# The output projection of a hybrid decoder trunk: seven block products in place of eight, accumulated in PSUM

## The chip, the cores and the metric

The kernel runs on one core of a Trainium2 chip. The metric is the device time of one execution in microseconds (us); lower is better. TensorE (PE), VectorE (DVE), ScalarE (ACT), GpSimd (POOL) and SyncE (SP, which here only issues transfers) work in order, each on its own queue, and wait for each other by semaphores.

## What is computed

Two layers (DEPTH = 2) over 1024 tokens of width 1024, all in float32. The part that matters, cut from the reference:

```python
for l in range(DEPTH):
    ...
    merged = jax.nn.sigmoid(gate_a) * y_a + jax.nn.sigmoid(gate_b) * y_b
    x = x + g1 * (merged @ w_out[l])
    h = rms_norm(x, norm2_g[l]) * (1.0 + sc2) + sh2
    x = x + g2 * ((jax.nn.silu(h @ w_gate[l]) * (h @ w_up[l])) @ w_down[l])
return rms_norm(x, final_g)
```

`merged @ w_out` is a 1024 x 1024 by 1024 x 1024 product. `c_act @ w_ada[l]` (the adaLN modulation) is computed for the next layer while the present one runs.

## The kernel before

Activations are held transposed: 128 channels on the partitions, tokens along the row, as 8 tiles of 128 x 1024 (KT = 8, HALF = 512 tokens). A float32 product is made of three passes of rounded operands: each operand is split into a high part (ScalarE's copy to a rounded type) and a low part (the remainder, by a subtraction on GpSimd for weights and mostly on VectorE for activations), and `products` (L707 to 712) issues high x high, high x low and low x high into one PSUM bank of 128 x 512.

**Merge.** For each of 8 channel tiles the two branch outputs come from 48 matmuls into four PSUM banks. VectorE multiplies them by the gates, which SP loads per tile (L1040), and adds them to `m_sum`; ScalarE makes `mg_hi` of it, VectorE `mg_lo`.

**Output projection** (units U_OUT to U_OUT+7). A unit is one tile of 128 output channels: SP loads its weights (L704), ScalarE splits off the high part (L685), GpSimd the low part (L693), one unit ahead. TensorE runs 8 inner tiles x 2 halves of the tokens x 3 passes = 48 matmuls a unit, 384 in all, two units alternating between PSUM banks 0 and 1, and 2 and 3. After each unit VectorE adds the bank pair, times g1, to `x_sb` (L2926). In layer 0 it then makes two or three of the 16 row reductions for the next layer's modulation (L2453), whose rows SP loads by ROWS_BEHIND. ScalarE squares the updated x (L1924), GpSimd sums the squares (L1183). The last two units run half by half: first both first halves, then both second halves, so that the norm of the first half (`mean_squares` L1394 on TensorE, the root on ScalarE, the reciprocal on VectorE, `norm_scale` L1403 on TensorE) is made under the second halves.

**Entry of the FFN.** The first gate and up products (`first_up`) take h of the first half as VectorE makes it, channel tile by channel tile (`hidden_scaled` L2570, `hidden_lo` L2581); the mean squares of the second half stand between them.

**Down projection.** Near the end of a layer the product with w_down already runs as seven products over 11 pairs of blocks, 77 steps of 12 matmuls each. Weights and hidden blocks, with their sums made earlier, are loaded step by step (SP, L1099 and L1112), split through a ring of three slots (`d_hi_lo`; copies L1912 on ScalarE, low halves on GpSimd L666 and VectorE L2441) and accumulated into 8 PSUM banks; `down_evictions` (from L3090) spreads the accumulations into x behind VectorE's low halves by a list of step numbers.

All orders are written out by hand, engine by engine; a counter a semaphore says how many instructions of a kind are done.

## Time and profile before

| what | value |
|---|---|
| median of 3 runs | 2896.54 us (2896.39 to 2897.36) |
| profiled execution | 2895.48 us |
| its span | 2893.6 us |
| granted TensorE clock, mean | 0.995 |
| busy: PE, DVE, ACT, POOL | 2829.5, 2103.5, 1223.9, 1253.3 us |

The profiled execution is one run beside the three; its span runs from the first to the last instruction, and its time has another 1.9 us around it. Busy times are sums over an engine's instructions: matmuls are pipelined, so the 0.39 us of a matmul's row is not the distance to the next. In the rows below "L709" is line 709 of the kernel, `out<-in` are the program's buffer names, "[1.57 <-PE ps L712]" is the idle time ahead of an instruction and what ended it, and PEclk is the granted TensorE clock as a share of 2.4 GHz.

### The profile page before, as it was taken

To read this page: it belongs to the slowest core of one execution; us is meant where nothing else is said; L and a number is where in the kernel's file an instruction comes from. 1 tells how busy PE (TensorE), PEld (TensorE's weight loads), DVE (VectorE), ACT (ScalarE), POOL (GpSimd) and SP (SyncE) were. 2 spreads that over 40 slices of the span, in tenths; PEclk is the share of its full clock that TensorE was granted. 3 is DMA by queue.
4 is the path that set the end of the run, shared out by engine and by line. 5 is a ranking of instruction groups with operands and counts; after the bars stand their busy time and mean duration, and the time that the engine had idled before them with its cause. 6 is when DMAs were issued, how large, how long until landed. Compare 5 with 4: busy or idle time off the path is not lost.

```text
span 2893.6 us, 38026 instructions
## 1 busy us (share of the span) xinstructions
PE 2829.5 (98%) x13924; PEld 2386.9 (82%) x13924; DVE 2103.5 (73%) x2575; ACT 1223.9 (42%) x1965; POOL 1253.3 (43%) x834
## 2 busy tenths in 40 slices
PE   6999999999999999999999999999999899999998
PEld 6888889988877888888878888898888788888887
DVE  7998688865687777757668896788533878776665
ACT  3433377762242333344542335778313333233443
POOL 0354322242535555554625452223223555555454
PEclk9999999999999999999999999999999999999999
DMA  7565400224615544466635652011351345544665
GB/s 293 166 195 177 152 16 13 51 50 155 223 51 192 169 170 164 153 199 217 198 131 160 186 177 74 17 23 41 106 175 44 122 158 174 180 163 155 196 196 167
DMA packets 332745, 408.59 MB, mean 141 GB/s; under 512 B 52369, under 2 KB 242961, under 8 KB 328338
## 3 DMA queue, kind: packets, MB, share of 16 engines
q1 hardware_dynamic: 290128, 298.41, 34.0%
q10 hardware_dynamic: 42434, 107.77, 10.0%
q8 instruction: 111, 1.82, 0.3%
q14 instruction: 72, 0.59, 0.1%
HBM read 299.33 MB, written 104.40 MB: 140 GB/s over the span
## 4 chain that ended last, share of the span: by engine, by line
PE 86%; DVE 6%; ACT 3%; DMA 2%; POOL 1%; issue 1%; SPq 0%; ACTq 0%; DVEq 0%; POOLq 0%
PE ps L709 15%; PE ps L711 15%; PE ps L712 15%; PE ps L1775 9%; PE ps L1777 9%; PE ps L1776 9%; PE ps L1635 4%; PE ps L1616 2%; PE ps L1656 2%; PE ps L1655 2%; PE ps L1621 2%; PE ps L1620 2%; DMA raw<-in_w_b_out 1%; DVE h_lo L2581 1%; DMA ada_rows<-in_w_ada 1%
## 5 line engine op out<-in xcount | busy, mean ns | idle before, releaser
L655 POOL TENSOR_TENSOR wlo<-blocks,whi 128x512 fp32r<-128x512 f32 x288 | 430.3, 1501 | 378.0 <-ACT whi L649 375.2
L693 POOL TENSOR_TENSOR wlo<-raw,whi 128x1024 fp32r<-128x1024 f32 (+4 forms) x156 | 236.4, 1532 | 706.3 <-ACT whi L685 706.2
L649 ACT ACTIVATE whi<-blocks 128x512 fp32r<-128x512 f32 x288 | 180.4, 627 | 316.9 <-PE ps L1777 254.1
L2441 DVE TENSOR_TENSOR d_hi_lo<-blocks,d_hi_lo 128x512 fp32r<-128x512 f32 x154 | 204.3, 1330 | 140.7 <-ACT d_hi_lo L1912 140.4
L666 POOL TENSOR_TENSOR d_hi_lo<-w_pair,d_hi_lo 128x512 fp32r<-128x512 f32 x148 | 203.4, 1377 | 199.4 <-ACT d_hi_lo L1912 199.4
L709 PE MATMUL ps<-h_hi,whi 128*128 128x512 f32 x832 | 281.6, 401 | 7.0 <-DVE h_lo L2581 5.5
L711 PE MATMUL ps<-h_lo,whi 128*128 128x512 f32 x832 | 274.5, 393 | 0.0
L712 PE MATMUL ps<-h_hi,wlo 128*128 128x512 f32 x832 | 273.4, 391 | 0.0
L685 ACT ACTIVATE whi<-raw 128x1024 fp32r<-128x1024 f32 (+4 forms) x162 | 106.9, 699 | 353.0 <-PE ps L712 292.3
L1775 PE MATMUL ps<-h_hi,whi 128*128 128x512 f32 x640 | 249.5, 390 | 5.3 <-issue 3.2
L1777 PE MATMUL ps<-h_hi,wlo 128*128 128x512 f32 x640 | 249.1, 389 | 0.0
L1776 PE MATMUL ps<-h_lo,whi 128*128 128x512 f32 x640 | 249.0, 389 | 0.0
L709 PE MATMUL ps<-d_hi_lo 128*128 128x512 f32 x616 | 240.4, 390 | 2.6 <-DVE d_hi_lo L2441 2.4
L711 PE MATMUL ps<-d_hi_lo 128*128 128x512 f32 x616 | 239.7, 389 | 0.0
L712 PE MATMUL ps<-d_hi_lo 128*128 128x512 f32 x616 | 239.7, 389 | 0.0
L1775 PE MATMUL ps<-e_hi,whi 128*128 128x512 f32 x480 | 187.7, 391 | 6.4 <-POOL wlo L655 6.4
L2441 DVE TENSOR_TENSOR pt_lo<-ps,pt_hi 128x512 fp32r<-128x512 f32 x256 | 164.6, 685 | 39.8 <-ACT pt_hi L1912 39.2
L709 PEld LDWEIGHTS ps<-h_hi,whi 128*128 128x128 f32 x832 | 154.2, 190 | 41.0 <-DVE h_lo L2581 9.8
L1777 PE MATMUL ps<-e_hi,wlo 128*128 128x512 f32 x480 | 187.2, 390 | 0.0
L1776 PE MATMUL ps<-e_lo,whi 128*128 128x512 f32 x480 | 187.2, 390 | 0.0
L712 PEld LDWEIGHTS ps<-h_hi,wlo 128*128 128x128 f32 x832 | 157.3, 189 | 34.0
L711 PEld LDWEIGHTS ps<-h_lo,whi 128*128 128x128 f32 x832 | 157.7, 190 | 33.2
(338 smaller groups left out, 6888.4 us busy)
## 6 DMA issues: line engine op xcount, KB each, us to landing
blocks<-hidden_scratch SPq DMA_DIRECT2D x154, 256.0 KB, 3.7
ada_raw<-in_w_ada SPq DMA_DIRECT2D x64, 512.0 KB, 4.2
raw<-in_w_in SPq DMA_DIRECT2D x92, 256.0 KB, 4.6
w_pair<-in_w_down SPq DMA_DIRECT2D x22, 1024.0 KB, 6.2
sums_scratch<-w_pair ACTq DMA_DIRECT2D x22, 1024.0 KB, 3.9
w_pair<-sums_scratch SPq DMA_DIRECT2D x88, 256.0 KB, 3.3
blocks<-in_w_gate SPq DMA_DIRECT2D x84, 256.0 KB, 3.2
blocks<-in_w_up SPq DMA_DIRECT2D x84, 256.0 KB, 3.0
```

The costliest lines, as they stand in the source:

```text
L649: act.activation(block_view(whi, s), blocks[:, r, :], ACT.Copy).then_inc(block_hi.sem, 1)
L655: pool.tensor_tensor(block_view(wlo, s), blocks[:, r, :], block_view(whi, s).bitcast(F32), ALU.subtract)\
L666: eng.tensor_tensor(d_tile(n, 0, 1), w_pair[:, n % 4, :], d_tile(n, 0, 0).bitcast(F32), ALU.subtract)\
L693: last = pool.tensor_tensor(dst(wlo[:, s, :]), src(raw[:, s, :]), dst(whi[:, s, :].bitcast(F32)), ALU.subtract)
L709: pe.matmul(o, w_h, x_h, start=first, stop=False, skip_group_check=added)
L711: pe.matmul(o, w_h, x_l, start=False, stop=False, skip_group_check=added)
L712: return [pe.matmul(o, w_l, x_h, start=False, stop=last, skip_group_check=added) for o, (x_h, _) in zip(outs, xs)]
L1635: last = pe.transpose(ps[:, 4 + t, k * P:(k + 1) * P], probs[:, T % 2, kt * P:(kt + 1) * P], ident[:, 0:P])
L1775: pe.matmul(bank, w_h, x_h, start=opens and j == 0, stop=False, skip_group_check=added)
L1776: pe.matmul(bank, w_h, x_l, start=False, stop=False, skip_group_check=added)
L1777: end = pe.matmul(bank, w_l, x_h, start=False, stop=(j == 3), skip_group_check=added)
L2441: return dve.tensor_tensor(out, value, hi.bitcast(F32), ALU.subtract)
```

## The change

The product merged @ w_out is cut into blocks of 128 inner rows by 512: pairs of inner tiles (OPAIRS = 4) give a11, a21, a12, a22 for the weights and b11, b12, b21, b22 for the merged activations. Seven products of sums of blocks (P1 to P7, in the order of OUT) replace the eight of blocks. Each product has a step per pair, n = 0 to 27, of 4 output tiles x 3 passes = 12 matmuls. Products accumulate into bank sets 0 to 3 or 4 to 7 (OUT_BANK), some into what the product before left there (those not in OUT_OPENS), and VectorE adds a bank to x between them (`out_eviction`).

- SP loads the four weight pairs during the merge; GpSimd makes the 16 weight sums there; VectorE makes the sums of the activations per merge tile. The plain blocks a11 are loaded behind the merge's last gates, a12 and a22 later.
- Steps 0 to 3 use the old weight slots; from step 4 on weights and activations pass through rings of three (`ow_ring`, `oh_ring`): ScalarE's copies of step n wait for TensorE's step n-3, GpSimd makes the low half of the weights, VectorE that of the activations.
- Squares of x and their sums, the mean squares and the norm's scale move to other places between the steps, and the first FFN products interleave the two units evenly.
- The next layer's 16 modulation reductions of layer 0 move to the down projection, behind every third step; SP loads their rows there.

The diff, cut to its core:

```diff
+    OPAIRS = KT // 2
+    OSTEPS = 7 * OPAIRS
+    OUT = ("P1", "P5", "P6", "P3", "P7", "P2", "P4")
+    OUT_HIDDEN = {"P5": 0, "P6": 1, "P3": 2, "P7": 3, "P2": 4, "P4": 5}
+    OUT_BANK = {"P1": 0, "P6": 0, "P7": 0, "P4": 0, "P5": 4, "P3": 4, "P2": 4}
+    OUT_OPENS = ("P1", "P5", "P2")
+    ADA_STEPS = 12
...
+        def out_weight(n):
+
+            p, j = divmod(n, OPAIRS)
+            name = OUT[p]
+            if name in ("P1", "P2"):
+                return raw[:, j // 2, (j % 2) * HALF:(j % 2 + 1) * HALF]
+            if name == "P4":
+                return out_a22[j // 2][:, j % 2, :]
+            return out_pair[j][:, {"P6": 0, "P7": 1, "P3": 2, "P5": 3}[name], :]
...
+                for j in range(OPAIRS):
+                    if j % 2 == 0:
+                        sp.wait_ge(w_lo_done.sem, w_lo_done.at(l, U_MERGE + KT - 1 + j // 2))
+                        apart(sp)
+                    load_out_block(j, 0, 0, raw_part(j))
...
+                def weight_sums(j):
+
+                    a11, a21, a12, a22 = (out_pair[j][:, n, :] for n in range(4))
+                    pool.wait_ge(wo_loaded.sem, wo_loaded.at(l, 16 * OPAIRS))
+                    pool.tensor_tensor(a22, a21, a22, ALU.add).then_inc(wo_sum.sem, 1)
+                    pool.tensor_tensor(a21, a11, a21, ALU.subtract).then_inc(wo_sum.sem, 1)
+                    pool.wait_ge(wo_sum.sem, wo_sum.at(l, 4 * j + 1))
+                    pool.tensor_tensor(a11, a22, a11, ALU.subtract).then_inc(wo_sum.sem, 1)
+                    pool.wait_ge(wo_sum.sem, wo_sum.at(l, 4 * j + 3))
+                    pool.tensor_tensor(a12, a12, a11, ALU.subtract).then_inc(wo_sum.sem, 1)
...
                 for n in range(1, KT):
                     split_lo(pool, l, U_MERGE + n)
-                split_lo(pool, l, U_OUT)
-                split_lo(pool, l, U_OUT + 1)
-                for n in range(KT - 2):
-                    split_lo(pool, l, U_OUT + n + 2)
-                    if n:
-                        for t in range(2):
-                            add_squares(l, 1, t, n)
-                add_squares(l, 1, 0, KT - 2)
-                add_squares(l, 1, 0, KT - 1)
-                split_lo(pool, l, U_FFN)
-                add_squares(l, 1, 1, KT - 2)
-                add_squares(l, 1, 1, KT - 1)
+                    if n >= 4:
+                        weight_sums(n - 4)
+                for n in range(OSTEPS):
+                    pool.wait_ge(wo_hi.sem, wo_hi.at(l, wo_hi_number(n, 0)))
+                    pool.tensor_tensor(ow_tile(n, 1), out_weight(n), ow_tile(n, 0).bitcast(F32), ALU.subtract)\
+                        .then_inc(wo_lo_w.sem, 1)
+                    if 21 <= n < 25:
+                        add_squares(l, 1, 0, n - 20)
+                    if n == 25:
+                        split_lo(pool, l, U_FFN)
+                split_lo(pool, l, U_FFN + 1)
+                for k in range(1, KT):
+                    add_squares(l, 1, 1, k)
...
+                def out_step(n):
+
+                    p, j = divmod(n, OPAIRS)
+                    if j == 0:
+                        if p < 2:
+                            wait(pe, mg_free, l, KT - 1 + p)
+                        else:
+                            pe.wait_ge(wo_ev.sem, wo_ev.at(l, 4 * (p - 1)))
+                    pe.wait_ge(wo_lo_w.sem, wo_lo_w.at(l, n + 1))
+                    if n < OPAIRS:
+                        pe.wait_ge(mg_ready.sem, mg_ready.at(l, n + 1))
+                    else:
+                        pe.wait_ge(wo_lo_h.sem, wo_lo_h.at(l, n - OPAIRS + 1))
+                    for m in range(4):
+                        end = out_product(n, m)
+                        if m == 3:
+                            end.then_inc(wo_used.sem, 1)
+                        elif n in (6 * OPAIRS - 1, 7 * OPAIRS - 1):
+                            end.then_inc(wo_end.sem, 1)
+                        if n == 6 * OPAIRS and m == 1:
+                            pe.wait_ge(wo_ev.sem, wo_ev.at(l, 20 + 3))
+                            mean_squares(l, 2)
+
+                for n in range(OSTEPS):
+                    out_step(n)
+                    if n == 6 * OPAIRS:
+                        norm_scale(l, 2)
...
+                def wo_hi_part(n):
+
+                    p, j = divmod(n, OPAIRS)
+                    if n < OPAIRS:
+                        act.wait_ge(wo_loaded.sem, wo_loaded.at(l, 2 * 16 * OPAIRS))
+                        wait(act, unit_used, l, U_MERGE + KT - 1 + n // 2)
+                    elif n < OPAIRS + 3:
+                        wait(act, unit_used, l, U_MERGE + KT)
+                    else:
+                        act.wait_ge(wo_used.sem, wo_used.at(l, n - 2))
...
+                    copy(ow_tile(n, 0), out_weight(n)).then_inc(wo_hi.sem, 1)
+                    if n >= OPAIRS:
+                        copy(oh_tile(n, 0), out_hidden(n)).then_inc(wo_hi.sem, 1)
+
+                def out_square(t, k):
+
+                    act.wait_ge(wo_ev.sem, wo_ev.at(l, (12, 20)[t] + k + 1))
+                    square(l, 1, t, k)
...
+                for n in range(2, 27):
+                    wo_hi_part(n)
+                    if 19 <= n < 23:
+                        out_square(0, n - 19)
+                    if n in (23, 24):
+                        for k in range(2):
+                            out_square(0, 2 * (n - 21) + k)
+                    if n == 25:
+                        split_hi(act, l, U_FFN)
                 norm_std(l, 2)
...
+                OUT_EVICTIONS = {8: ((0, 0), (0, 1)), 9: ((0, 2), (0, 3)), 11: ((1, 0),), 12: ((1, 1),), 13: ((1, 2), (1, 3)),
+                                 14: ((2, 0),), 15: ((2, 1),), 16: ((2, 2),), 17: ((2, 3),),
+                                 18: ((3, 0),), 19: ((3, 1),), 20: ((3, 2),), 21: ((3, 3),),
+                                 22: ((4, 0), (4, 1)), 23: ((4, 2), (4, 3))}
...
+                for n in range(OPAIRS, OSTEPS - 2):
+                    out_hidden_low(n)
+                    if n in (8, 11):
+                        wait(dve, x_back[n // 11], l, 16)
+                    for p, m in OUT_EVICTIONS.get(n, ()):
+                        out_eviction(p, m)
+                    if n == 24:
+                        squares_added(0, 5)
+                squares_added(0, 6)
+                squares_added(0, 7)
+                for m in range(4):
+                    out_eviction(5, m, True)
+                out_hidden_low(OSTEPS - 2)
                 norm_inverse(l, 2)
...
+                    if l + 1 < DEPTH and n >= ADA_STEPS and n % 3 == 0 and n < ADA_STEPS + 6 * KT:
+                        at = (n - ADA_STEPS) // 3
+                        if at == 0:
+                            wait(dve, c_loaded, l, 32)
+                        ada_product(l, 4 * KT + at, at // KT, next_raw, next_c)
```

The orders on VectorE and ScalarE change in places that the diff shows only as conditions. **VectorE from the first ring steps on (layer 0)**; `oh_ring<-mg_raw` is a low half, `x_sb<-ps` an accumulation of a finished bank. Before:

```order
L2926 SCALAR_TENSOR_TENSOR x_sb<-ps,mod,x_sb 128x1024 [waits x_back_first,unit_used]
L2453 ISA next_raw,mod<-next_raw,next_c 128x1024 [waits c_loaded,ada0_loaded]
L2453 ISA mod 128x1
L2453 ISA next_raw,mod<-next_raw,next_c 128x1024 [waits ada1_loaded]
L2453 ISA mod 128x1
```

Now:

```order
L2564 TENSOR_TENSOR oh_ring<-mg_raw,oh_ring 128x512 [waits wo_hi_then_block_hi_then_d_hi] x5
L3075 SCALAR_TENSOR_TENSOR x_sb<-ps,mod,x_sb 128x512 [waits wo_used_then_plain_done_then_d_used,x_back_first]
L3075 SCALAR_TENSOR_TENSOR x_sb<-ps,mod,x_sb 128x512 [waits wo_used_then_plain_done_then_d_used]
L2564 TENSOR_TENSOR oh_ring<-mg_raw,oh_ring 128x512 [waits wo_hi_then_block_hi_then_d_hi]
L3075 SCALAR_TENSOR_TENSOR x_sb<-ps,mod,x_sb 128x512 [waits wo_used_then_plain_done_then_d_used] x2
L2564 TENSOR_TENSOR oh_ring<-mg_raw,oh_ring 128x512 [waits wo_hi_then_block_hi_then_d_hi] x2
```

The first group of five low halves is for steps 4 to 8; P1's four accumulations stand two behind the low half of step 8 and two behind that of step 9.

**VectorE around the start of P4 (steps 24 to 27)**; `sq_sum` is a sum of squares. Before, at the end of the projection:

```order
L2467 TENSOR_TENSOR mod<-mod,cols 128x8 [waits ada_used] x2
L2938 SCALAR_TENSOR_TENSOR a_57<-mod,cols 128x8 [waits mod_ready]
L2967 SCALAR_TENSOR_TENSOR x_sb<-ps,mod,x_sb 128x512 [waits out_half] x2
L2558 RECIPROCAL rstd<-std 128x4 [waits std_ready]
L2967 SCALAR_TENSOR_TENSOR x_sb<-ps,mod,x_sb 128x512 [waits unit_used]
```

Now:

```order
L2564 TENSOR_TENSOR oh_ring<-mg_raw,oh_ring 128x512 [waits wo_hi_then_block_hi_then_d_hi]
L3101 TENSOR_TENSOR sq_sum<-sq_sum,sq_ring 128x512 [waits sq0_added,sq0_ready]
L2564 TENSOR_TENSOR oh_ring<-mg_raw,oh_ring 128x512 [waits wo_hi_then_block_hi_then_d_hi]
L3101 TENSOR_TENSOR sq_sum<-sq_sum,sq_ring 128x512 [waits sq0_added,sq0_ready] x2
L3075 SCALAR_TENSOR_TENSOR x_sb<-ps,mod,x_sb 128x512 [waits wo_ev_then_w_pair_sum_then_d_ev,wo_end] x3
L3075 SCALAR_TENSOR_TENSOR x_sb<-ps,mod,x_sb 128x512 [waits wo_ev_then_w_pair_sum_then_d_ev,wo_used_then_plain_done_then_d_used]
L2564 TENSOR_TENSOR oh_ring<-mg_raw,oh_ring 128x512 [waits wo_hi_then_block_hi_then_d_hi]
L2681 RECIPROCAL rstd<-std 128x4 [waits std_ready]
L2564 TENSOR_TENSOR oh_ring<-mg_raw,oh_ring 128x512 [waits wo_hi_then_block_hi_then_d_hi]
```

The low halves here are of steps 24, 25, 26 and 27; VectorE took over three of the sums of squares, and P2's four accumulations stand behind them and behind the low half of step 25.

**ScalarE over steps 23 to 27**; `ow_ring` and `oh_ring` are the two copies of a step, `sq_ring` a square. Before, for the last units:

```order
L685 ACTIVATE whi<-raw 128x1024 [waits unit_used,raw1_loaded]
L1924 ACTIVATE sq_ring<-x_sb 128x512 [waits sq0_added,wo_ev]
L1924 ACTIVATE sq_ring<-x_sb 128x512 [waits sq1_added]
L1924 ACTIVATE sq_ring<-x_sb 128x512 [waits sq0_added,wo_ev] x2
L1946 ACT_TABLE_LOAD
```

Now:

```order
L2006 ACTIVATE ow_ring<-raw 128x512 [waits wo_loaded,wo_used_then_plain_done_then_d_used]
L2006 ACTIVATE oh_ring<-mg_raw 128x512
L2018 ACTIVATE sq_ring<-x_sb 128x512 [waits sq0_added,wo_ev_then_w_pair_sum_then_d_ev] x2
L2006 ACTIVATE ow_ring<-out_a_low 128x512 [waits wo_used_then_plain_done_then_d_used]
L2006 ACTIVATE oh_ring<-mg_raw 128x512
L2018 ACTIVATE sq_ring<-x_sb 128x512 [waits sq0_added,wo_ev_then_w_pair_sum_then_d_ev] x2
L2006 ACTIVATE ow_ring<-out_a_low 128x512 [waits wo_used_then_plain_done_then_d_used]
L2006 ACTIVATE oh_ring<-mg_raw 128x512
L734 ACTIVATE whi<-raw 128x1024 [waits wo_used_then_plain_done_then_d_used,raw0_loaded]
```

Two squares now stand between the copies of step 23 and those of 24, and two more ahead of those of 25. A square waits until the square two earlier, which used its ring slot, is in the sum.

## Rows read from the trace of the kernel before

**Rows 1.** The page's chain that ended last, by engine.

```profile
PE 86%; DVE 6%; ACT 3%; DMA 2%; POOL 1%; issue 1%; SPq 0%; ACTq 0%; DVEq 0%; POOLq 0%
```

**Rows 2.** Windows by stage: merge, out, FFN entry, down, layer 1's out.

```profile
core 0: us, PE busy (x) PEld busy (x) DVE busy (x) ACT busy (x) POOL busy (x), PEclk, DMA share, GB/s
638.00:725.00 87.00, 86.93 (x384) 71.67 (x383) 45.92 (x33) 19.02 (x18) 20.12 (x9) 1.00 0.47 154
725.00:814.00 89.00, 89.00 (x402) 73.94 (x401) 56.52 (x56) 22.13 (x30) 51.27 (x21) 1.00 0.62 199
814.00:885.00 71.00, 64.19 (x277) 50.57 (x276) 61.40 (x74) 31.30 (x52) 31.05 (x21) 0.98 0.25 84
1250.00:1440.00 190.00, 189.43 (x837) 156.57 (x836) 124.43 (x110) 89.70 (x156) 106.02 (x77) 1.00 0.70 217
2139.00:2228.00 89.00, 89.00 (x402) 73.95 (x401) 21.27 (x21) 22.13 (x30) 35.95 (x21) 1.00 0.31 101
```

**Rows 3.** Timeline of PE, layer 0's out stage: start, us, what.

```profile
724.92 0.62 PE L709 MATMUL ps<-mg_hi,whi 128*128 128x512 f32 x2
...
804.48 0.95 PE L1394 MATMUL ps<-columns,sq_sum 128*128 128x1 f32 x8
805.29 0.49 PE L709 MATMUL ps<-mg_hi,whi 128*128 128x512 f32 x1
...
813.85 0.39 PE L709 MATMUL ps<-h_hi,whi 128*128 128x512 f32 x1
```

**Rows 4.** Timeline of all engines, one step of the down projection.

```profile
1338.67 0.39 PE L709 MATMUL ps<-d_hi_lo 128*128 128x512 f32 x1
...
1338.93 0.63 ACT L1912 ACTIVATE d_hi_lo<-w_pair 128x512 fp32r<-128x512 f32 x1 [1.57 <-PE ps L712]
...
1339.64 1.29 POOL L666 TENSOR_TENSOR d_hi_lo<-w_pair,d_hi_lo 128x512 fp32r<-128x512 f32 x1 [1.43 <-ACT d_hi_lo L1912]
...
1340.12 1.36 DVE L2441 TENSOR_TENSOR d_hi_lo<-blocks,d_hi_lo 128x512 fp32r<-128x512 f32 x1 [1.36 <-ACT d_hi_lo L1912]
...
1341.59 0.75 DVE L3085 SCALAR_TENSOR_TENSOR x_sb<-ps,mod,x_sb 128x512 f32<-128x512 f32 x1
```

**Rows 5.** SP's timeline, then DMA GB/s over 705 to 726 us.

```profile
716.79 0.81 SPq L1040 DMA_DIRECT2D gl<-gate_scratch  x2
...
GB/s 0 0 0 133 148 382 273 390 460 314 312 344 207 32 0 0 0 0 0 0 0 0 0 0 156 335 304 312 406 395 259 260 258 349 311 363 358 296 327 247
```

**Rows 6.** Timeline of POOL: one sum of squares, alone.

```profile
799.99 1.29 POOL L1183 TENSOR_TENSOR sq_sum<-sq_sum,sq_ring 128x512 f32<-128x512 f32 x1 [1.43 <-ACT sq_ring L1924]
```

**Rows 7.** Weight splits on POOL, reductions on DVE; their group over 725:814.

```profile
726.26 2.40 POOL L693 TENSOR_TENSOR wlo<-raw,whi 128x1024 fp32r<-128x1024 f32 x1 [8.48 <-ACT whi L685]
...
737.20 3.50 POOL L693 TENSOR_TENSOR wlo<-raw,whi 128x1024 fp32r<-128x1024 f32 x1 [8.54 <-ACT whi L685]
...
738.36 3.42 DVE L2453 CUSTOM_DVE_ANT_0 next_raw<-next_raw,next_c 128x1024 f32<-128x1024 f32 x1
...
L2453 DVE CUSTOM_DVE_ANT_0 next_raw<-next_raw,next_c 128x1024 f32<-128x1024 f32 x16 | 33.5, 2123 | 2.7 <-DMA next_raw<-in_w_ada 2.7
```

**Rows 8.** PE behind its longest waits in the FFN entries, and windows there.

```profile
872.61 0.76 PE L1775 MATMUL ps<-e_hi,whi 128*128 128x512 f32 x1 [3.18 <-POOL wlo L655]
...
2286.59 0.47 PE L1775 MATMUL ps<-e_hi,whi 128*128 128x512 f32 x1 [3.20 <-POOL wlo L655]
...
873.00:875.00 2.00, 2.00 (x6) 1.52 (x6) 2.00 (x2) 0.00 (x0) 2.00 (x2) 0.50 0.90 356
2287.00:2290.00 3.00, 3.00 (x15) 2.47 (x14) 3.00 (x3) 0.00 (x0) 3.00 (x3) 1.00 0.87 304
```

**Rows 9.** FFN entry: mean squares on PE, first second-half h on DVE.

```profile
819.20 0.95 PE L1394 MATMUL ps<-columns,sq_sum 128*128 128x1 f32 x8
...
824.63 1.41 DVE L2570 SCALAR_TENSOR_TENSOR t_late<-x_sb,a,ps 128x512 f32<-128x512 f32 x2 [1.37 <-PE ps L1403]
```

**Rows 10.** Timeline of DVE near step 29 of the down projection.

```profile
1328.41 2.44 DVE L3085 SCALAR_TENSOR_TENSOR x_sb<-u_part,mod,x_sb 128x512 f32<-128x512 f32 x2
```

More of the change, by code:

```diff
@@ L440, in trunk @@
         h_ready = count("h_ready", 4 * KT)
-        out_half = count("out_half", 2)
+        wo_end = count("wo_end", 6)
         pcol_ready = count("pcol_ready", 1)
@@ new lines, in _ @@
+                for j in range(OPAIRS):
+                    if j % 2 == 0:
+                        sp.wait_ge(w_lo_done.sem, w_lo_done.at(l, U_MERGE + KT - 1 + j // 2))
+                        apart(sp)
+                    load_out_block(j, 0, 0, raw_part(j))
+                sp.wait_ge(wo_loaded.sem, wo_loaded.at(l, 2 * 16 * OPAIRS))
+                wait(sp, unit_used, l, U_MERGE + KT)
+                apart(sp)
+                for j in range(OPAIRS):
+                    sp.wait_ge(wo_lo_w.sem, wo_lo_w.at(l, j + 1))
+                    apart(sp)
+                    load_out_block(j, 0, 1, raw_part(j))
@@ new lines, in _ @@
+                sp.wait_ge(mg_comb.sem, mg_comb.at(l, 4 * OPAIRS))
+                apart(sp)
+                for j in range(OPAIRS):
+                    load_out_block(j, 1, 1, out_a22[j // 2][:, j % 2, :])
+                for n in range(2):
+                    sp.wait_ge(wo_lo_w.sem, wo_lo_w.at(l, 5 * OPAIRS + 2 * n + 2))
+                    apart(sp)
+                    up_unit(n)
+                sp.wait_ge(wo_lo_w.sem, wo_lo_w.at(l, 3 * OPAIRS + 4))
+                apart(sp)
+                for name in PLAIN_BLOCKS:
+                    load_block(name, 1)
@@ L1727, in _ @@
                     end[1].then_inc(unit_used.sem, 1)
-                for n in range(KT - 2):
-                    unit_ready(pe, l, U_OUT + n)
-                    wait(pe, wo_ev, l, n - 1)
-                    for k in range(KT):
-                        if n == 0:
-                            wait(pe, mg_ready, l, KT if k == KT - 1 else KT - 1)
-                        end = tile_products(pe, n % 2, 2 * (n % 2), mg_hi, mg_lo, [(k, k)],
-                                            first=(k == 0), last=(k == KT - 1))
-                    end[1].then_inc(unit_used.sem, 1)
@@ L2243, in _ @@
+                table(ACT.Sqrt)
+                for n in range(2):
+                    wo_hi_part(n)
+                wait(act, unit_used, l, U_MERGE + KT)
                 wait(act, x_spilled, l, 16)
[L2244 removed]
+                for part, tiles in enumerate((slice(0, 4), slice(4, KT))):
                     act.dma_start(x_sb[:, tiles, :], xs_dram[:, tiles, :]).then_inc(x_back[part].sem, 16)
[L2246 to L2254 removed]
@@ L3187, in _ @@
                     down_evictions(n)
+                    if l + 1 < DEPTH and n >= ADA_STEPS and n % 3 == 0 and n < ADA_STEPS + 6 * KT:
[3 more added lines that the diff above has]
+                        ada_product(l, 4 * KT + at, at // KT, next_raw, next_c)
+                    if l + 1 < DEPTH and n == 60:
+                        for m in range(2):
+                            modulation(l, 4 + m, m, cols[:, l + 1, m * KT:(m + 1) * KT])
+                        wait(dve, mod_ready, l, 6)
+                        apart(dve)
+                        dve.scalar_tensor_tensor(a1[:, :], mod[:, 1, :], 1.0, cols[:, l + 1, ROW_N1:ROW_N1 + KT],
+                                                 ALU.add, ALU.mult).then_inc(a1_ready.sem, 1)
                     if l + 1 < DEPTH and n in (40, 42):
```

308 lines of the change are left out of this document (168 added, 140 removed).

## The prediction

> **What bounds the kernel now.** I read the page's chain first [rows 1]: TensorE holds 86% of the chain that ended last. Then the windows by stage [rows 2]: in the output projection (725 to 814 in layer 0, 2139 to 2228 in layer 1) TensorE is busy in 89.00 of 89 us, both times with 402 instructions. The matmul timeline [rows 3] prices it: the first product of the stage starts at 724.92, the first of the next stage at 813.85, 88.93 later. A matmul starts every 0.2267 us (the merge runs its 384 in 87 us, [rows 2]); the 0.39 of a row is latency, not pace. 384 of them are 87.05, the two insertions for the norm 0.81 each (804.48 to 805.29, and one like it): 88.67 of the 88.93. The stage has no wait to remove. Only fewer matmuls shorten it, and any new wait of TensorE lengthens it one for one.
>
> Two more views matter. The down projection already runs seven block products through a ring of three, and shows the rhythm of a step [rows 4]. The entry of the FFN (814 to 885) is the one stage where TensorE idles (64.19 busy of 71, [rows 2]).
>
> **The change, part by part (per layer).**
> *Matmuls.* 28 steps of 12 are 336 for 384: 48 x 0.2267 = **-10.88**.
>
> *Rhythm of a step.* With S the start of a step (1338.67), ScalarE's two copies for the step two later start at S+0.26, GpSimd's low half ends at S+2.26, VectorE's low half, held back until GpSimd is through, at S+2.81, and an accumulation into x behind it takes 0.75 [rows 4], or 0.67 apart in a row (two like it in 1.41, [rows 9]). A step lasts 2.72, so low halves come 2.6 before they are needed. Inside a product nothing is lost; that cover is 2.6 and no more.
>
> *Sums of weight blocks.* 16 x 1.29 (a 128x512 subtraction, [rows 4]) = 21 on GpSimd, which is busy 20 of 87 us in the merge [rows 2]: cost 0. Without that cover the merge's weight splits would be late. VectorE's combinations, three of 1.36 at most in a tile of 10.9 us, fit beside its 46 busy of 87.
>
> *Start.* The four A11 blocks stand on SP's queue behind the last gates. Those issue from 716.79 for 0.81 [rows 5]; 1 MB of gates and 1 MB of blocks at some 320 GB/s (the middle of that answer's bandwidth row) end near 724.4. ScalarE (0.63) and GpSimd (1.29) follow, so step 0 starts near 726.5: **+1.5** (0 to 2.5). Before, the first weights had landed long since.
>
> *Banks.* Steps 8, 12, 16 and 20 may start only when four accumulations of an earlier product are done, and VectorE's queue has the last of them behind the low half of a *later* step (9, 13, 17, 21). The low half of step 9 ends at S(7)+2.81; two accumulations behind it end at S(7)+4.07, where step 8 was due at S(7)+2.72: 1.40 lost with the hand-over of 0.05. Step 12 loses the same; steps 16 and 20, with one accumulation behind, 0.74 each: **+4.3** (2.8 to 5).
>
> *Start of P4 (step 24), the largest term.* After half of step 24 TensorE waits for the third accumulation of P2 and the whole sum of squares, then writes the mean squares. Squares and sums are now threaded between steps on three queues. Count from S(19)=0; steps 20 to 24 are due at 3.46, 6.18, 8.90, 11.62, 14.34. GpSimd adds square 1 behind low half 21, to 4.10 (1.29 alone, [rows 6]); only then may ScalarE (0.63 for 128x512, [rows 4]) overwrite the ring slot, so copies 22 start at 4.69, not 3.72. The next rounds: add 2 ends 8.53, low half 23 9.82, add 3 11.66, square 5 12.34, low half 24 14.24 (VectorE's 14.79, so step 24 starts 0.5 late), add 4 16.08, VectorE's add 5 16.85, square 7 17.5. Copies 25 stand behind square 7: 17.45 to 18.62, VectorE's low half 20.00. Behind *that* on VectorE stand adds 6 and 7 and the four accumulations of P2. TensorE reaches the wait at 16.21. If VectorE's work comes in a row, the third accumulation ends at 23.2, a wait of 7.0. But GpSimd asks at 19.65 for the split of the next weights, and two such instructions take turns: GpSimd's split from 737.20 took 3.50 instead of 2.40, and VectorE's reduction issued at 738.36 took 3.42, ending 1.08 after GpSimd did [rows 7]. So split to 22.40, add 6 to 22.95, low half 26 to 24.24, add 7 to 24.80, third accumulation 26.8: a wait of 10.6. I take turns, as those rows do: **+11.1** with the 0.5 (7.5 to 12.5).
>
> *Clock.* After a wait of 3.18 us in layer 0 the granted clock was 0.50 (1.2 GHz) from 873 to 875: six matmuls at half pace, 6 x 0.2 = 1.2 us lost; after 3.20 in layer 1 it stayed 1.00 (2.4 GHz) [rows 8]. The new wait is longer than either: **+1.2** (0 to 1.7).
> The Trainium skill (TensorE: Matmul & The Clock Gate, "What's actually happening") says that an idle array falls to 1.2 GHz and rises again only after it has been kept busy, which speaks against any change that trades matmuls for one long wait. By it both layers pay, as in my sum; by the layer 1 row alone the forecast would be 2.4 less.
>
> *Entry of the FFN.* Before, most squares of the second half of the sequence were added while the last tiles ran; mean squares started 5.35 after the stage (819.20) and the first second-half h at 10.78 (824.63) [rows 9]. Now all seven adds follow the last weight split on GpSimd, in turns with VectorE's low halves of h. The same count from S(25), with the stage's end at 8.16, ends these adds at 8.8, 10.8, 12.1, 14.0, 15.9, 17.7 and 19.6; mean squares wait until 11.4 after the stage, then 0.81, root and reciprocal 0.4, the matmuls queued ahead 1.36, scale 0.8, first h at 14.9. From there VectorE sets the pace as before: **+4.1** (2 to 6).
>
> *Once, in layer 0.* The 16 reductions for the next layer (33.5 of VectorE, [rows 7]) leave a stage where they were free for the down projection, where VectorE has 124 busy of 190 [rows 2]. On a plain step one costs nothing (low half 0.3 late, cover 2.6). At steps 27 to 30 VectorE already runs back to back, its two accumulations alone 2.44 of the 2.72 [rows 10], and reductions after 27 and 30 push low half 31 to about 0.6 past its need. Each also holds SP's queue, with the next weight and hidden loads behind it, until VectorE's reduction two earlier is done; those loads then land about when needed. **+1** (0 to 6).
>
> **Sum.** -10.88 + 1.5 + 4.3 + 11.1 + 1.2 + 4.1 = +11.3 a layer, +22.6 for two, +1: +23.6. The profiled execution took 2895.48 (span 2893.6), so 2919.1; the median of the three runs is 1.06 above that execution: **2920**. With every low end it is +1.4 a layer, 2899; with every high end +16.8 a layer and 6, 2936.
>
> **Rivals.** *Cover holds.* Slower turns into faster if the queues run ahead of my count: if VectorE's adds 6 and 7 and three accumulations are done when step 24 is half through. The price of P4's start and the clock is then 0, the entry's 1, and -10.88 + 1.5 + 4.3 + 1 = -4.1 a layer: 2889 with the +1; without the bank waits too, 2880. It decides at a chain shorter by 7.0. For it speaks the down projection, which loses almost nothing; against it, its accumulations stand a whole product behind, not one step. *A draw.* The wait at P4 is 2.5 and the entry costs 2, start and banks as in my sum, the clock stays: -0.6 a layer, 2896. It needs squares that don't hold back ScalarE's copies. *The down projection becomes the bound in layer 0*: each of 16 reductions costs 1.2 (1.08 of work and a hand-over) on the path through SP's queue: +19 more, 2938 or above. Against it: SP loads four slots ahead, 10.9 us of steps. *The sums come late* or the matmuls are not fewer: the order of instructions shows 336 a layer, and the last sums behind the last merge split, which stood two units (21.8 us) ahead of the one at 726.26 [rows 7]: 704.5 + 2.40 + 4 x 1.29 is near 712, 24 before step 4 wants its first. I give it nothing of its own.
>
> **How the numbers follow.** 0.2% (5.8 us) is about what a measurement of this kernel can tell from no change. My sum with its ends 0.68, cover holds 0.15, draw 0.10, down projection 0.07. Faster by over 0.2% is the second: 0.15; within 0.2%: 0.10; slower: 0.75. The range takes my sum's ends, the draw and the upper half of the second case: 2887 to 2935.
>
> **What would show it.** Right: out stages of about 96 us instead of 88.93, with TensorE waits on VectorE's accumulations of 1.4, 1.4, 0.7, 0.7 and one of 7 to 11 before the mean squares, a granted clock below 1 just behind it, and first second-half h some 15 behind the stage. Wrong: no wait over 3 us in the out stage (then the cover held), or the time lost in the down projection of layer 0.

## The result, and the profile after

The changed kernel takes 2929.4 us (median of 4 runs, 2927.02 to 2936.4) against 2896.95 (4 runs beside it): the ratio is 1.0113, 95% interval 1.0094 to 1.0133. Slower was forecast, at 2920; the loss is 32 us, not 23.6. The profiled execution of after took 2927.96, its span is 2925.8 (2893.6 before).

From the timelines of TensorE, each stretch from the first product of a stage to the first of the next:

| stretch | before | after, layer 0 | after, layer 1 | change | forecast a layer |
|---|---|---|---|---|---|
| merge, up to the first output product | 87.40; 88.13 | 90.41 | 90.97 | +3.01; +2.84 | +1.5 |
| output projection | 88.93 | 95.46 | 97.63 | +6.53; +8.70 | +5.7 |
| FFN, up to the first down product | 436.93 | 441.12 | 440.66 | +4.19; +3.73 | +4.1 |
| layer 0's down projection, up to layer 1's first product | 214.26 | 218.46 | | +4.20 | +1 |

These are 33.2; the rest of the program is 1.0 shorter, in all 32.2, the difference of the spans.

Windows of after over the two output projections (before: [rows 2]) and over what follows their waits:

```profile
core 0: us, PE busy (x) PEld busy (x) DVE busy (x) ACT busy (x) POOL busy (x), PEclk, DMA share, GB/s
725.00:822.00 97.00, 82.13 (x354) 66.30 (x353) 67.70 (x66) 38.34 (x67) 52.07 (x35) 0.95 0.24 87
808.00:810.00 2.00, 1.45 (x7) 1.45 (x8) 1.75 (x3) 0.00 (x0) 0.00 (x0) 0.50 0.00 0
810.00:812.00 2.00, 2.00 (x6) 1.71 (x7) 0.18 (x1) 0.26 (x1) 0.00 (x0) 0.50 0.00 0
834.00:838.00 4.00, 4.00 (x16) 3.42 (x17) 2.23 (x4) 3.08 (x5) 0.00 (x0) 0.57 0.00 0
2154.00:2250.00 96.00, 80.60 (x337) 64.91 (x336) 63.90 (x62) 37.14 (x66) 48.31 (x33) 0.91 0.25 91
2158.00:2162.00 4.00, 4.00 (x12) 3.09 (x12) 3.86 (x4) 3.00 (x6) 4.00 (x3) 0.57 1.02 434
2241.00:2243.00 2.00, 2.00 (x9) 2.00 (x10) 1.18 (x2) 0.12 (x1) 0.00 (x0) 0.50 0.00 0
2243.00:2247.00 4.00, 4.00 (x15) 3.42 (x14) 0.35 (x2) 1.50 (x4) 0.65 (x1) 0.50 0.00 0
```

TensorE was never idle in this stage; now it is busy in 82 of 97 us. Its timeline in layer 0 shows where, with the idle time before each product in brackets:

```profile
692.56 0.73 PE L758 MATMUL ps<-o_hi,whi 128*128 128x512 f32 x2 [1.47 <-POOL wlo L742]
...
726.94 0.47 PE L758 MATMUL ps<-mg_hi,whi 128*128 128x512 f32 x1 [1.44 <-issue]
...
750.20 0.50 PE L758 MATMUL ps<-oh_ring,ow_ring 128*128 128x512 f32 x1 [1.25 <-DVE x_sb L3075]
...
762.62 0.50 PE L758 MATMUL ps<-oh_ring,ow_ring 128*128 128x512 f32 x1 [1.24 <-DVE x_sb L3075]
...
774.37 0.50 PE L758 MATMUL ps<-oh_ring,ow_ring 128*128 128x512 f32 x1 [0.58 <-DVE x_sb L3075]
...
786.17 0.50 PE L758 MATMUL ps<-oh_ring,ow_ring 128*128 128x512 f32 x1 [0.58 <-DVE x_sb L3075]
...
808.55 1.87 PE L1477 MATMUL ps<-columns,sq_sum 128*128 128x1 f32 x8 [9.77 <-DVE x_sb L3075]
...
822.40 0.39 PE L758 MATMUL ps<-h_hi,whi 128*128 128x512 f32 x1
...
833.05 1.05 PE L1477 MATMUL ps<-columns,sq_sum 128*128 128x1 f32 x8 [2.74 <-POOL sq_sum L1254]
```

In order: a wait in the merge that I had not forecast (1.47, for a weight split on GpSimd), the start (1.44), the four waits for banks (3.65 together), the wait before the mean squares (9.77), and the late squares in the FFN's entry (2.74). Layer 1 has the same list, with 1.98 at the start.

What VectorE and GpSimd do ahead of the 9.77, from their timelines:

```profile
798.27 0.69 DVE L3101 TENSOR_TENSOR sq_sum<-sq_sum,sq_ring 128x512 f32<-128x512 f32 x1 [1.25 <-POOL sq_sum L1254]
...
802.02 4.49 DVE L3101 TENSOR_TENSOR sq_sum<-sq_sum,sq_ring 128x512 f32<-128x512 f32 x2
806.44 2.71 DVE L3075 SCALAR_TENSOR_TENSOR x_sb<-ps,mod,x_sb 128x512 f32<-128x512 f32 x4
```

```profile
801.75 2.55 POOL L742 TENSOR_TENSOR wlo<-raw,whi 128x1024 fp32r<-128x1024 f32 x1 [0.19 <-ACT whi L734]
804.26 1.71 POOL L1423 TENSOR_TENSOR ow_ring<-out_a_up,ow_ring 128x512 fp32r<-128x512 f32 x1
```

The addition of square 5 takes 0.69, with GpSimd idle. The two additions of squares 6 and 7 take 4.49 us, beside the split of the next stage's weights; only then come the accumulations of P2, whose third TensorE waits for.

The merge's wait, on GpSimd: it stands until 682.76 for the last block loads, then makes four sums at 1.6 to 2.3 us each, and the split that TensorE needs comes behind them. A sum takes 1.29 alone, but here VectorE's combinations run beside them:

```profile
682.76 2.31 POOL L1410 TENSOR_TENSOR out_tables<-out_tables 128x512 f32<-128x512 f32 x1 [9.79 <-DMA out_last<-in_w_out]
...
688.55 1.61 POOL L1415 TENSOR_TENSOR out_tables<-out_tables 128x512 f32<-128x512 f32 x1
...
690.13 2.37 POOL L742 TENSOR_TENSOR wlo<-raw,whi 128x1024 fp32r<-128x1024 f32 x1
```

Layer 0's down projection: a reduction on a free step, then VectorE's backlog at the doubled accumulations (before, without a reduction: [rows 10]), and TensorE behind it:

```profile
1294.31 1.21 DVE L2576 CUSTOM_DVE_ANT_0 next_raw<-next_raw,next_c 128x1024 f32<-128x1024 f32 x1
...
1345.27 2.44 DVE L3252 SCALAR_TENSOR_TENSOR x_sb<-u_part,mod,x_sb 128x512 f32<-128x512 f32 x2
1347.63 2.31 DVE L2576 CUSTOM_DVE_ANT_0 next_raw<-next_raw,next_c 128x1024 f32<-128x1024 f32 x1
1349.87 2.97 DVE L2564 TENSOR_TENSOR d_hi_lo<-blocks,d_hi_lo 128x512 fp32r<-128x512 f32 x3
```

```profile
1350.70 0.47 PE L758 MATMUL ps<-d_hi_lo 128*128 128x512 f32 x1 [1.41 <-DVE d_hi_lo L2564]
```

### The profile page after: what moved, and what is told of

Read it like the earlier page. It is cut to its first block, busy times and chain, and to the rows that moved or that the text cites. A ratio compares the mean times of both kernels' runs of the same rounds, so it can differ in the third digit from the quotient of the medians.

```text
span 2925.8 us, 38063 instructions
## 1 busy us (share of the span) xinstructions
PE 2825.0 (97%) x13828; PEld 2377.7 (81%) x13828; DVE 2208.4 (75%) x2687; ACT 1252.1 (43%) x2045; POOL 1340.6 (46%) x902
## 4 chain that ended last, share of the span: by engine, by line
PE 82%; DVE 6%; POOL 3%; ACT 3%; issue 2%; DMA 2%; SPq 0%; ACTq 0%; DVEq 0%; POOLq 0%
PE ps L758 14%; PE ps L760 13%; PE ps L761 13%; PE ps L1869 9%; PE ps L1870 8%; PE ps L1871 8%; PE ps L1718 4%; PE ps L1738 2%; PE ps L1739 2%; PE ps L1699 2%; PE ps L1704 2%; PE ps L1703 2%; POOL sq_sum L1254 1%; DVE d_hi_lo L2564 1%; DMA ada_rows<-in_w_ada 1%
## 5 line engine op out<-in xcount | busy, mean ns | idle before, releaser
L742 POOL TENSOR_TENSOR wlo<-raw,whi 128x1024 fp32r<-128x1024 f32 (+4 forms) x142 | 198.4, 1415 | 546.5 <-ACT whi L734 546.4
L713 POOL TENSOR_TENSOR d_hi_lo<-w_pair,d_hi_lo 128x512 fp32r<-128x512 f32 x148 | 210.2, 1423 | 196.2 <-ACT d_hi_lo L2006 196.1
L734 ACT ACTIVATE whi<-raw 128x1024 fp32r<-128x1024 f32 (+4 forms) x146 | 89.8, 658 | 274.9 <-PE ps L761 213.3
```

Of the source, the lines that this page charges most:

```text
L713: eng.tensor_tensor(d_tile(n, 0, 1), w_pair[:, n % 4, :], d_tile(n, 0, 0).bitcast(F32), ALU.subtract)\
L742: last = pool.tensor_tensor(dst(wlo[:, s, :]), src(raw[:, s, :]), dst(whi[:, s, :].bitcast(F32)), ALU.subtract)
```

## The experiments

The theory: each loss is a wait at a place of its own, set by the order in which something stands on VectorE's, GpSimd's, ScalarE's or SP's queue; move it and the time comes back. The rival: the queues around the output projection are full, and a wait that is taken away comes back at the next place. All ratios are to the kernel before, on the same chip.

**e1: ask for the mean squares later.**

```diff
-    if n == 6 * OPAIRS and m == 1:      # mean squares in step 24
+    if n == 6 * OPAIRS + 2 and m == 1:  # step 26; low halves 26, 27 ahead of P2's accumulations, ScalarE's copies 27 ahead of the root
```

> Changed kernel, but TensorE writes the mean squares of the first half two steps later (in step 26 instead of step 24), and VectorE makes the low halves 26 and 27 ahead of P2's accumulations. Theory (the wait is one of place: TensorE asks for something that the queues finish 9.8 us later, while it has two more steps of work at hand): the wait of 9.8 us falls to 2 to 4 us, the clock stays up, the next stage starts 8 to 10 us sooner and some of that is lost at its entry: 12 to 18 us less in all, 2912 to 2918. Rival (the chain of squares is the bound, wherever TensorE waits for it): the out stage gets shorter by as much, but the first h of the FFN comes no sooner, the same time is waited there: 0 to 5 us less, 2925 to 2930.

2929.04 us, 1.0111 (1.0094 to 1.0128): nothing gained, the rival's case. TensorE's timeline in layer 0:

```profile
803.46 0.47 PE L758 MATMUL ps<-oh_ring,ow_ring 128*128 128x512 f32 x1 [2.11 <-DVE oh_ring L2564]
...
812.12 1.87 PE L1477 MATMUL ps<-columns,sq_sum 128*128 128x1 f32 x8 [2.71 <-DVE x_sb L3075]
...
824.70 0.47 PE L758 MATMUL ps<-h_hi,whi 128*128 128x512 f32 x1 [3.41 <-issue]
```

The 9.77 are now 2.11 for a low half, 2.71 for the mean squares and 3.41 for the first h of the FFN. So the chain of squares sets the time, not the place where TensorE asks for its end.

**e2: accumulations one step earlier.** Every entry of OUT_EVICTIONS, the squares and their sums move up by one low half.

```diff
-  OUT_EVICTIONS = {8: ((0, 0), (0, 1)), 9: ((0, 2), (0, 3)), 11: ((1, 0),), ...
+  OUT_EVICTIONS = {7: ((0, 0), (0, 1)), 8: ((0, 2), (0, 3)), 10: ((1, 0),), ...
```

> Changed kernel, but every accumulation into x stands one low half earlier on VectorE's queue, and with them the squares on ScalarE and their sums on GpSimd. Theory (the last accumulation of a product stands behind a low half that comes too late): the four waits for banks, 1.25, 1.24, 0.58, 0.58 us, go to 0, which is 3.7 us a layer, and the wait before the mean squares gets shorter by one step, 2.7: together 6.4 a layer, 13 in all, 2916. Rival (the squares go in lockstep with the copies and low halves, one round of the three queues at a time, and an earlier start is lost in the round): the bank waits go, the wait of 9.8 stays: 7 us less, 2922. Second rival (the first accumulations now wait for x to come back from memory): a new wait at step 8, nothing won there.

2917.35, 1.0070 (1.0053 to 1.0087), 12 us less than the changed kernel, near the theory's 13. The four waits for banks are gone. The wait before the mean squares is 3.6 shorter, but 2.8 of that are new waits for low halves (0.71 and 2.07), so part of the earlier start is lost in the round, as the rival says. The longest left in layer 0, the third line being ScalarE's:

```profile
796.48 0.47 PE L758 MATMUL ps<-oh_ring,ow_ring 128*128 128x512 f32 x1 [2.07 <-DVE oh_ring L2564]
...
804.47 1.87 PE L1477 MATMUL ps<-columns,sq_sum 128*128 128x1 f32 x8 [6.14 <-DVE x_sb L3075]
```

```profile
780.92 0.63 ACT L2018 ACTIVATE sq_ring<-x_sb 128x512 f32<-128x512 f32 x1 [2.63 <-POOL sq_sum L1254]
```

ScalarE waits 2.63 for GpSimd's sum before it may overwrite a slot of the ring, and the copies for the next step are queued behind that square. This is the lockstep that the prediction counted through.

**e3: the reductions on other steps.**

```diff
+  ADA_AT = (12, 14, 16, 18, 20, 22, 33, 35, 38, 40, 42, 44, 54, 56, 58, 60)
-  n % 3 == 0 and n < ADA_STEPS + 6 * KT
+  n in ADA_AT           # VectorE; SP issues the load at step n + 1
```

> Changed kernel, but the 16 reductions of the next layer's modulation stand on steps of the down projection that have few accumulations (none at 24 to 32, 45 to 53), and SP issues their loads one step behind instead of three ahead. Theory (VectorE's backlog at steps 27 to 31 and 45 to 53 makes the low halves late): layer 0's down projection is as long as before the change, 4.2 us less, 2925. Rival (a reduction costs time wherever it stands in this stage, through GpSimd's and VectorE's turns or through the loads): 0 to 1 us less, 2928 to 2930.

2922.98, 1.0084 (1.0067 to 1.0101). Layer 0's down projection is 215.22 (218.46 in the changed kernel, 214.26 before): 3.2 of the 4.2 come back. The waits of 1.41, 0.62, 0.27 and 0.40 that the changed kernel has there are gone, one of 0.73 is new. The 3.2 is not a steady figure: e1, e2, e4, e5, e6 and e11 leave this stage as it is in the changed kernel, and it lasts 216.5 to 219.3 in them; with the reductions moved (e3, e7, e9, e10) it lasts 215.2 to 216.1. So the reductions cost 2.2 to 5.1 where the change puts them, and 0.9 to 1.8 on the other steps. The medians say 6.4, more than the stage can give.

**e4: the sums of weight blocks one unit later**, the last four behind the low half of step 1 (`if n >= 5: weight_sums(n - 5)`).

> Changed kernel, but GpSimd makes the first sums of weight blocks one merge unit later, and the last four behind the low halves of steps 0 and 1. Theory (GpSimd stood waiting for the block loads, then did four sums ahead of a weight split that was due, and so the merge waits 1.47 us in each layer): the wait goes, 1.6 us a layer, 3.2 in all, 2926. Rival (the four sums are only moved onto steps 0 to 3): the wait goes from the merge and one of 1 to 3 us appears at steps 2 or 4: no change, 2929.

2934.85, 1.0131 (1.0114 to 1.0148): slower by some 5. The merge's wait went, and a larger one came, as the rival says:

```profile
735.34 0.50 PE L758 MATMUL ps<-mg_hi,whi 128*128 128x512 f32 x1 [4.04 <-POOL wlo L1423]
```

**e5: a ring of four for the squares**, on top of e2.

```diff
+  def sq_slot(occ, t, k): return (2 * t + k) % 4 if occ else 2 * t + k % 2
-  if 20 <= n < 24:      # GpSimd's squares 1 to 4 (with e2)
+  if 20 <= n < 25:      # 1 to 5; VectorE 6 and 7; mean squares in step 25
```

> The kernel with early accumulations, and: the squares of the two halves share a ring of four slots where each had two, GpSimd adds the squares 1 to 5 and VectorE 6 and 7, the mean squares are written one step later (in step 25), and ScalarE's copies 27 and the split of the second weight unit stand ahead of the root. Theory (a ring of two slots makes ScalarE wait for GpSimd's sums, 2.6 us at a time, with the copies for the next steps queued behind): no wait over 1 us is left in the out stage, it lasts 79 to 82 us (91.3 with early accumulations alone), the next stage waits no longer than before the change: 18 to 24 us less than early accumulations alone, 2893 to 2899. Rival (GpSimd's low half and sum, 1.29 + 1.75 = 3.04 us a step against 2.72, are the bound, whatever the ring): waits of 1 to 2 us move to the low halves of steps 22 to 26: 8 us less, 2909.

2900.32, 1.0010 (1.0001 to 1.0020): 17 less than e2, from several moves at once (the ring, the step of the mean squares, who adds which square, ScalarE's order). The out stages are 85.10 and 84.21, not 79 to 82. What is left are two waits, for the third accumulation of P2 and for the reciprocal, both on VectorE's queue:

```profile
799.62 1.05 PE L1481 MATMUL ps<-columns,sq_sum 128*128 128x1 f32 x8 [2.29 <-DVE x_sb L3086]
...
804.65 2.08 PE L1490 MATMUL ps<-ident,rstd 128*128 128x128 f32 x8 [1.89 <-DVE rstd L2692]
```

No low half is late any more, so the rival (GpSimd's 3.04 a step) falls.

**e6: the first A11 blocks ahead of the last gates**, with e4's later sums (the last four behind step 3).

```diff
+  if t == KT - 1:
+      for j in range(2): load_out_block(j, 0, 0, raw_part(j))
```

> Changed kernel, but the first two A11 blocks are loaded ahead of the last gates, GpSimd's sums of weight blocks stand one merge unit later, and the last four behind the low half of step 3. Theory (the wait at the start, 1.44 and 1.98 us, is for the A11 blocks that stand behind the gates; the wait of 1.47 us in the merge is for a split behind four sums): both go, 2.9 us in layer 0 and 3.5 in layer 1, 6 to 7 in all, 2923. Rival (the four sums behind step 3 take 5.2 to 7 us and make low half 4 late): 2 to 4 us come back at step 4 in each layer: 2927 to 2931.

2928.54, 1.0108 (1.0091 to 1.0124). TensorE has no wait in the merge and none at the start, so the start was SP's order; but step 4 now waits 2.90 for its low half, behind the last four sums, and the stage is 99.04 in layer 0. The rival again.

```profile
739.55 0.47 PE L758 MATMUL ps<-oh_ring,ow_ring 128*128 128x512 f32 x1 [2.90 <-POOL ow_ring L1428]
```

**e7: the edits of e2, e3, e5 and e6 together.**

> All repairs together: early accumulations, ring of four and late mean squares, early A11 blocks and late sums, reductions on free steps. Theory (the losses were waits at separate places, so the repairs add): 2896 of the ring of four, less 6 at the starts and 4 in layer 0's down projection: 2884 to 2890, below the kernel before. Rival (GpSimd and VectorE are saturated around the output projection, and a wait removed comes back at the next place): 2896 to 2905, not below it.

2900.74, 1.0012 (1.0003 to 1.0022): the rival. The starts have no wait and the down projection is 215.16, but the wait of 2.90 at step 4 is in, and the two of e5 stay (2.30; 0.42 in layer 0, 2.50 in layer 1).

**e8: SP's loads for the reductions three steps later**, the reductions in place (`0 <= n // 3 - 4 < 2 * KT`).

> Changed kernel, but SP issues the load for each of the 16 reductions three steps later, and the reductions stay where they are. Theory (VectorE's backlog makes the low halves late): no change, 2929, and the waits of 1.41 and 0.62 us in layer 0's down projection stay. Rival (SP stands waiting for the reduction two earlier with the loads of the next steps queued behind): the waits go, 3 to 4 us less, 2925.

2930.28, 1.0109 (1.0092 to 1.0126). The waits of 1.41, 0.27 and 0.40 are 1.20, 0.27 and 0.42; only the one of 0.62 went, and the stage is 217.59. In the changed kernel ScalarE's copies had waited for loads of hidden blocks, here the longest:

```profile
1355.40 0.63 ACT L2006 ACTIVATE d_hi_lo<-w_pair 128x512 fp32r<-128x512 f32 x1 [4.87 <-DMA blocks<-hidden_scratch]
```

In e8 these waits are gone, and the stage still lasts 3.3 more than before the change. So VectorE's backlog costs that much with SP out of it. That SP adds to it isn't shown: 217.59 lies within the 216.5 to 219.3 of the runs that leave the loads where they are.

**e9: three more moves on e7.** VectorE makes the first pair's sums behind merge tile 4; the gate unit's split goes behind step 27; second-half squares in pairs.

> All repairs, and three more moves: VectorE makes the first pair's four sums of weight blocks in the merge (GpSimd's last four then end before the output projection), GpSimd's split of the first gate weights stands behind the low half of step 27, and ScalarE squares two tiles at a time for the second half. Theory (what is left in the out stage is order and the turns of GpSimd and VectorE: 2.90 us at step 4, 2.30 us before the mean squares, 0.4 to 2.5 us at the scale, and the clock at 1.2 GHz behind them): these waits go, the clock stays up, the out stages last 78 to 80 us against 88.93 before the change; with entries as before: 2872 to 2880, faster than the kernel before by 0.7 to 0.9%. Rival (the splits of both gate units, 4.8 us, now end later than the stage and TensorE waits at the FFN's entry instead): 2882 to 2892.

2901.61, 1.0013 (1.0003 to 1.0022): a miss, by a new wait that neither theory named. GpSimd waited for VectorE's sums, and a merge split behind it was late:

```profile
701.19 1.29 POOL L1419 TENSOR_TENSOR out_tables<-out_tables 128x512 f32<-128x512 f32 x1 [15.19 <-DVE out_tables L3086]
```

```profile
708.67 1.22 PE L758 MATMUL ps<-o_hi,whi 128*128 128x512 f32 x2 [4.55 <-POOL wlo L742]
```

The out stages got to 84.3, the FFN back to 437.07 and 437.03.

**e10: the two places of e9 mended.** ScalarE's root also stands ahead of its first squares of the second half, which the expectation doesn't name.

```diff
-  if t == 4: first_weight_sums()     # VectorE
+  if t == 3: first_weight_sums()
-  squares_added(0, 6); squares_added(0, 7)   # VectorE
+  for k in (6, 7):                           # TensorE, from the ring
+      pe.matmul(ps[:, 6, t:t + 1], sq_ring[:, sq_slot(1, 0, k), ...], mean_col, start=False, ...)
```

> The last version, with VectorE's four sums of weight blocks behind merge tile 3 in place of 4, and TensorE taking the squares 6 and 7 of the first half straight from the ring (8 products of one column each more) in place of VectorE's two additions. Theory (the merge's new wait of 4.55 us was GpSimd waiting for VectorE's sums; the waits of 1.18 and 2.04 us in the out stage were VectorE's queue of additions, accumulations and low halves behind the last square): no wait over 0.5 us from the merge to the FFN's entry, the merge at 87.4 us, the out stages at 79 to 80 against 88.93 before the change, the clock at 1.00 through them: 16 to 20 us less than the kernel before, 2878 to 2883. Rival (VectorE and GpSimd slow each other by turns, and the work is only pushed on): one wait of 2 to 3 us stays in each layer, with 2 to 3 us at the lower clock behind it: 2886 to 2892.

2883.17 (5 runs), 0.9956 (0.9943 to 0.9970): faster than both kernels, 12 us below the one before and some 46 below the changed one. Its windows over the merge, the out stage and the FFN's entry of layer 0, and layer 1's out stage:

```profile
638.00:725.00 87.00, 87.00 (x386) 72.03 (x385) 58.02 (x48) 15.46 (x18) 38.78 (x21) 1.00 0.56 194
725.00:805.00 80.00, 79.84 (x369) 66.34 (x368) 61.88 (x64) 39.70 (x69) 54.02 (x36) 1.00 0.30 106
805.00:878.00 73.00, 66.94 (x280) 52.27 (x279) 63.39 (x77) 31.39 (x54) 34.91 (x24) 0.95 0.24 83
2138.00:2219.00 81.00, 80.11 (x366) 65.72 (x365) 63.02 (x67) 39.03 (x67) 55.44 (x39) 1.00 0.24 87
```

TensorE is busy throughout both out stages again, at 1.00; they last 80.26 and 80.23, 8.7 less than before. The time is just past the far end of what was expected: the FFN stretches are still 0.7 to 1.0 longer than before, the down projection 1.8.

So the queues have room in all for the smaller product. The rival held for e4, e6, e7 and e9, each time because a move filled one queue at one place, and it fell here. Whether TensorE's part in the squares or the root's place took away the waits of 1.18 and 2.04 in the out stage isn't separated.

**e11: only the gate unit's split moved**, in the changed kernel (behind step 27).

> Changed kernel, but GpSimd's split of the first gate weights stands behind the low half of step 27 instead of step 25: it no longer runs beside VectorE's additions of squares 6 and 7. Theory (the two engines take turns, and the split of 2.55 us is what stretches these two additions from 1.4 to 4.49 us): the additions take 1.4 to 2.7, the accumulations behind them start 2 to 3 us sooner, the wait before the mean squares is 7 to 8 us instead of 9.77; 2 us less a layer, less what the later split costs the FFN's entry: 2924 to 2928. Rival (the additions are late because their squares are, not for the split): the wait stays within 0.7 us of 9.77.

2928.05, 1.0107 (1.0090 to 1.0124).

```profile
805.14 2.35 DVE L3100 TENSOR_TENSOR sq_sum<-sq_sum,sq_ring 128x512 f32<-128x512 f32 x2
```

```profile
809.51 0.80 PE L1476 MATMUL ps<-columns,sq_sum 128*128 128x1 f32 x3 [7.61 <-DVE x_sb L3074]
...
825.15 0.47 PE L758 MATMUL ps<-h_hi,whi 128*128 128x512 f32 x1 [1.93 <-issue]
```

The additions take 2.35 instead of 4.49, and the wait 7.61 instead of 9.77: the split beside the additions was worth 2.2. The FFN's entry gives it back (1.93 and 0.38, for the weights split later), so the time stays.

## Why the prediction was right, and where its sizes were off

**Matmuls, -10.88: right.** With the waits gone (e10; one of 0.16 is left) the stage is 8.7 shorter than before, and 1.8 of the 2.2 missing are the one-column products: with squares 6 and 7 they take from 794.31 to 796.90 in its timeline, 2.6 where an insertion took 0.81.

```profile
794.31 0.95 PE L1496 MATMUL ps<-columns,sq_sum 128*128 128x1 f32 x8
795.12 1.93 PE L1501 MATMUL ps<-columns,sq_ring 128*128 128x1 f32 x16
796.90 0.49 PE L758 MATMUL ps<-oh_ring,ow_ring 128*128 128x512 f32 x1
```

**Banks, +4.3: right, a little large.** 1.25, 1.24, 0.58, 0.58 measured for 1.40, 1.40, 0.74, 0.74. Its 4.07 doesn't follow from its own rows: 2.81 + 0.67 + 0.75 is 4.23, which would make the term 4.9 and not 4.3, further off. e2 shows the cause to be the order: one place up, and all four are gone.

**Start of P4, +11.1: right, at 9.8.** The forecast was 10.6 and 0.5 for a late step 24; the step was on time and the wait is 9.77. The choice between turns (10.6) and VectorE's work in a row (7.0) is settled by e11: without the split beside the additions it is 7.61. That ScalarE's squares hold back the copies is seen in e2's row (2.63 <-POOL sq_sum). In e5, with the deeper ring, the late low halves are gone, but other moves came with it.

**Clock, +1.2: too small.** From the mean squares to the FFN's first product stand 42 matmuls and two insertions, 42 x 0.2267 + 2 x 0.81 = 11.1; they took 13.85 in layer 0 and 14.40 in layer 1, so 2.7 and 3.3 were lost, at a granted clock of 0.50 (1.2 GHz). I had priced it from [rows 8], six matmuls behind a wait of 3.2; here the low clock lasted longer, some 5 us behind the wait in layer 0 and 6 in layer 1. The prediction cites the Trainium skill (TensorE: Matmul & The Clock Gate, "What's actually happening") for an idle array falling to 1.2 GHz; the trace agrees, both layers pay. And layer 1 pays a second time, behind its start (0.57 from 2158 to 2162): P1's 48 matmuls took 12.59 there, 10.97 in layer 0.

**Start, +1.5: right** (1.44 and 1.98; e6 and e10 show the cause).

**Sums of weight blocks, 0: wrong.** The step failed on two points: it priced a sum at 1.29, alone, where VectorE's combinations beside it make it 1.6 to 2.3, and it took GpSimd's free time as one pool, where the first four sums waited for the loads and ran into a split that was due. It cost a wait of 1.47 in each layer. Of the prediction's rival *the sums come late* this is the part that came true, at a place that it didn't name: it counted the last sums, and the first were late.

**FFN's entry, +4.1: right** (4.19 and 3.73), partly by luck. The mean squares came 10.65 behind the stage (833.05), where 11.4 was forecast, but from there to the first second-half h it took 5.05, where the sum has 3.5; before the change it had been 5.43 by [rows 9]. So h came 15.7 behind the stage, 14.9 forecast.

```profile
838.10 1.41 DVE L2693 SCALAR_TENSOR_TENSOR t_late<-x_sb,a,ps 128x512 f32<-128x512 f32 x2 [1.31 <-PE ps L1486]
```

**Reductions in layer 0, +1 (0 to 6): too small**, 4.2. The prediction named the place, steps 27 to 31, but took one low half to be 0.6 late; the reductions there took 2.31 each instead of the 1.21 of a free step, and the wait is 1.41. The size is not steady: in e1, e4, e6 and e11 only the first of the two took 2.31, the second 1.21 or 1.22, and the wait is 0.37 to 0.39. e3 takes the wait away by moving the reductions, and e8 shows that it stays without SP.

So what is missing, 32.2 - 23.6 = 8.6, is mainly three terms: 5.2 of clock (1.5 and 2.1 more than forecast behind the mean squares, 1.6 at layer 1's start), 3.2 of reductions (in this execution) and 2.9 of sums. A smaller one is that each wait costs more than its idle time: in layer 0's out stage 78.05 (88.93 - 10.88), 3.65, 9.77 and 2.7 make 94.2, and it lasts 95.46. Against them stand the wait at P4 and the banks, 4.0 too high, both layers together.

The rivals: *cover holds* fell, with a wait of 9.77, *a draw* with it (it needed 2.5), and *the down projection becomes the bound* with a loss of 4.2 there instead of some 20. But what the change can give is there: e10 does the same 336 matmuls and is 0.44% faster than the kernel before.

## What to carry to other kernels

When matmuls are taken from a stage that TensorE fills, the other engines get less time for work that has grown. Count each engine's queue to the end of the stage: the largest wait here stood in the last product, where work for the next stage came beside it. A short ring that passes work through three engines hands one engine's wait on to the others; here moving the consumer alone gained nothing (e1), and the kernels with the deeper ring gained (e5, e10). A move within busy queues has to be counted at its new place too (e4, e6, e9).
